# Paired heads in the grouped-query attention, and the squares of the residual norms added on GpSimd ahead of one sum on TensorE

## What is computed

```python
def rmsnorm(x, g):
    y = x * lax.rsqrt(jnp.mean(x * x, axis=-1, keepdims=True) + 1e-6)
    return y * g
...
# 16 query heads, 4 key and value heads, head dimension 64
sc = jnp.einsum('bgrqd,bgkd->bgrqk', qblk, k) * scale
p = jax.nn.softmax(sc, axis=-1)
o = jnp.einsum('bgrqk,bgkd->bgrqd', p, v)
...
x = x + o_all_heads @ w_o
```

## Time and profile before

| | |
|---|---|
| median of 3 runs | 1263.02 us (1260.88 to 1265.97) |
| the profiled execution | 1267.91 us, span 1266.1 us |
| mean granted TensorE clock | 0.963 of 2.4 GHz |
| TensorE matmuls | 1173.1 us busy, 93% of the span, 8610 records |
| VectorE / ScalarE / GpSimd | 764.2 us (60%) / 620.1 us (49%) / 141.3 us (11%) |
| the chain that ended last | TensorE 76%, GpSimd 11%, VectorE 6%, ScalarE 4% |

### The profile page before, as it was taken

How to read it: one execution, slowest core, us unless ns; L and a number is a source line. 1 busy time by engine, 2 the same in 40 slices (tenths; PEclk the granted TensorE clock), 3 DMA queues, 4 the chain that set the end, 5 groups by cost and what they waited for, 6 DMA issues and landing times.

```text
span 1266.1 us, 22011 instructions
## 1 busy us (share of the span) xinstructions
PE 1173.1 (93%) x8610; PEld 1084.8 (86%) x8610; DVE 764.2 (60%) x1164; ACT 620.1 (49%) x1101; POOL 141.3 (11%) x236
## 2 busy tenths in 40 slices
PE   4987879899999999989988899999989999999997
PEld 4876758798999999989955699999978569999997
DVE  3699883355456666546455466656656546656653
ACT  5543325455455545554454355545554455554553
POOL 1399992000000000000000000000000000000000
PEclk8988879899999999999998899999999799999999
DMA  7424112244266665536430066656776104566550
GB/s 244 137 97 150 50 34 81 86 134 133 77 195 171 199 198 171 182 103 183 127 92 1 19 182 177 184 170 168 197 149 143 42 1 135 166 199 193 172 165 33
DMA packets 218142, 169.05 MB, mean 134 GB/s; under 512 B 20787, under 2 KB 208098, under 8 KB 217954
## 3 DMA queue, kind: packets, MB, share of 16 engines
q1 hardware_dynamic: 216962, 164.44, 44.5%
q0 software_dynamic: 496, 2.43, 0.5%
q10 hardware_dynamic: 624, 1.35, 0.4%
HBM read 167.15 MB, written 1.05 MB: 133 GB/s over the span
## 4 chain that ended last, share of the span: by engine, by line
PE 76%; POOL 11%; DVE 6%; ACT 4%; issue 2%; SPq 1%; DMA 1%; DVEq 0%; ACTq 0%; POOLq 0%
PE bank L1847 20%; PE bank L1849 20%; PE bank L1848 20%; PE bank L1913 11%; POOL arena L698 4%; POOL arena L737 2%; DVE wlo L1272 2%; POOL arena L738 1%; ACT whi L766 1%; PE bank L2198 1%; DVE arena L1265 1%; PE bank L1907 1%; PE bank L1909 1%; PE bank L1908 1%; POOL arena L719 1%
## 5 line engine op out<-in xcount | busy, mean ns | idle before, releaser
L1847 PE MATMUL bank<-mem_hi,whi 128*128 128x256 f32 x1408 | 407.4, 289 | 6.5 <-DVE mem_lo L1565 4.9
L1848 PE MATMUL bank<-mem_lo,whi 128*128 128x256 f32 x1408 | 400.4, 284 | 0.0
L1849 PE MATMUL bank<-mem_hi,wlo 128*128 128x256 f32 x1408 | 400.3, 284 | 0.0
L1847 PEld LDWEIGHTS bank<-mem_hi,whi 128*128 128x128 f32 x1408 | 272.2, 193 | 9.2 <-issue 8.5
L1847 PE MATMUL bank<-act_hi,whi 128*128 128x256 f32 (+1 forms) x920 | 267.0, 290 | 12.7 <-DVE act_lo L1291 4.7
L1848 PEld LDWEIGHTS bank<-mem_lo,whi 128*128 128x128 f32 x1408 | 272.0, 193 | 1.9 <-issue 1.4
L1849 PEld LDWEIGHTS bank<-mem_hi,wlo 128*128 128x128 f32 x1408 | 272.0, 193 | 0.0
L1848 PE MATMUL bank<-act_lo,whi 128*128 128x256 f32 (+1 forms) x920 | 261.6, 284 | 0.0
L1849 PE MATMUL bank<-act_hi,wlo 128*128 128x256 f32 (+1 forms) x920 | 261.5, 284 | 0.0
L1272 DVE TENSOR_TENSOR wlo<-raw,whi 128x1024 fp32r<-128x1024 f32 (+3 forms) x137 | 159.0, 1205 | 109.2 <-ACT whi L766 107.7
L1640 DVE TENSOR_TENSOR wlo<-raw,whi 128x1024 fp32r<-128x1024 f32 x177 | 208.9, 1221 | 3.8
(11 more groups left out here) (196 smaller groups left out, 1154.6 us busy)
## 6 DMA issues: line engine op xcount, KB each, us to landing
raw<-in_ffn_w_in_dram SPq DMA_DIRECT2D x132, 512.0 KB, 5.2
raw<-in_ffn_w_out_dram SPq DMA_DIRECT2D x33, 1024.0 KB, 5.0
raw<-in_w_in_ab_dram SPq DMA_DIRECT2D x11, 1024.0 KB, 5.4
raw<-in_w_in_dram SPq DMA_DIRECT2D x9, 1024.0 KB, 7.2
raw<-in_xa_wk_dram SPq DMA_DIRECT2D x4, 1024.0 KB, 5.7
raw<-in_xa_wv_dram SPq DMA_DIRECT2D x4, 1024.0 KB, 5.1
raw<-in_w_out_dram SPq DMA_DIRECT2D x4, 1024.0 KB, 5.0
raw<-in_xa_wq_dram SPq DMA_DIRECT2D x4, 1024.0 KB, 5.0
```

The costliest lines, as they stand in the source:

```text
L1847: pe.matmul(dst, w[0], a[0], start=start, stop=False, **kw)
L1848: pe.matmul(dst, w[0], a[1], start=False, stop=False, **kw)
L1849: return pe.matmul(dst, w[1], a[0], start=False, stop=stop, **kw)
```

## The change

There are two parts, made together.

**Norms 2 to 7.** ScalarE writes the squares of each pair of tiles into the two hf buffers in place of sq. GpSimd adds the four squared pairs into x_sum (three 128x512 additions) and then the halves of x_sum (one 128x256 addition), and TensorE sums that over the partitions by a single 128x256 matmul (`norm_sum`), in place of the eight. It stands behind the second cross-attention query tile (norm 2), behind the fourth k-step of the second half of the first hidden tile (norms 3, 5, 7), right behind the four abreast latent tiles (norm 4), and behind the first query tile (norm 6). GpSimd's load of the late constants stands behind its work for norm 3. In the tails of feed-forwards 0 and 1, VectorE issues x_low of a tile right behind the next tile's addition, not in pairs one pair later.

**Attention.** `attend_pairs` takes the 16 heads as 8 pairs. The score matmuls of the two halves alternate into two of four banks, the value matmuls alternate into the two halves of one bank (6 or 7), the transposes use banks 4 and 5. VectorE scales both heads by one reciprocal and one 1024-wide multiplication. There are four sets of probabilities in an area of their own. Scores of a pair wait for the exponentials of the pair two before it, from the third pair on. `keep_clock` is still issued ahead of the first transposes.

The diff, cut to its core (indentation reduced):

```diff
 grot = room(2, T)
+gprobs = room(4, TT, T, at=0)
+gprobsT = room(4, TT, T)
...
 x_rms_col = sb("x_rms_col", [P, 2, 2])
+x_sum = sb("x_sum", [P, 512])
...
 def score_bank(a):
-    return bank[(a + 2) % 3 if a < 12 else a % 3]
+    return bank[(a + 2) % 3 if a < 12 else a % 4]
...
             step(ins_)
-    pool.wait_ge(s_res, 2 * KC)
+    def add_squares(n):
+        at_ = 4 * (n - 2)
+        half = (x_sum[:, 0:T], x_sum[:, T:2 * T])
+        pool.wait_ge(s_xsq, at_ + 2)
+        if n > 2:
+            pool.wait_ge(s_xss, n - 2)
+        pool.tensor_tensor(x_sum[:], hf[:, 0, :], hf[:, 1, :], ALU.add).then_inc(s_acc, 1)
+        for j in range(2):
+            pool.wait_ge(s_xsq, at_ + 3 + j)
+            pool.wait_ge(s_acc, at_ + 1 + j)
+            pool.tensor_tensor(x_sum[:], x_sum[:], hf[:, j, :], ALU.add).then_inc(s_acc, 1)
+        pool.wait_ge(s_acc, at_ + 3)
+        pool.tensor_tensor(half[0], half[0], half[1], ALU.add).then_inc(s_acc, 1)
+    add_squares(2)
+    add_squares(3)
     pool.dma_start(late, consts[:, early_consts:]).then_inc(s_late, 16)
+    for n in range(4, 8):
+        add_squares(n)
...
         k, ss = stat_no["norm", n], bank[4][:, 0:T]
-        act.wait_ge(s_ss, SQ["norm", n] + 4)
+        act.wait_ge(s_xss, n - 1)
...
            .then_inc(s_hhi, 1)
+    def x_squares(n, j):
+        src = xT[:, 2 * j:2 * j + 2, :].rearrange("p c t -> p (c t)")
+        if n == 8:
+            squares(("norm", n), j, src, 512)
+        else:
+            if j >= 2:
+                act.wait_ge(s_acc, 4 * (n - 2) + j - 1)
+            elif n > 2:
+                act.wait_ge(s_acc, 4 * (n - 3) + 2 + j)
+            act.activation(hf[:, j % 2, :], src, ACT.Square).then_inc(s_xsq, 1)
             if m % 2:
-                squares(("norm", n), m // 2, xT[:, m - 1:m + 1, :].rearrange("p c t -> p (c t)"), 512)
+                x_squares(n, m // 2)
...
         evacuate("gv", i, gv[:, i, :], scale=x_rms_col[:, i, 0:1])
-    attend(12, 16, probs, probsT, GQA_UNITS)
+    def attend_pairs(first, pairs):
+        for i in range(pairs + 3):
+            for half in range(2):
+                a = first + 2 * i + half
+                if i < pairs:
+                    act.wait_ge(s_max, a + 1)
+                    if i >= 2:
+                        act.wait_ge(s_pt, a - 3)
+                    for t in range(TT):
+                        e = act.activation(gprobs[:, a % 4, t, :], score_bank(a)[:, t * T:t * T + T], ACT.Exp,
+                                           bias=nmax[:, a, t:t + 1], accum_out=rsum[:, a, t:t + 1])
+                    e.then_inc(s_exp, 1)
+            for half in range(2):
+                a = first + 2 * (i - 2) + half
+                if 2 <= i < pairs + 2:
+                    act.wait_ge(s_pt, a + 1)
+                    if i >= 4:
+                        act.wait_ge(s_o, a - 3)
+                    act.activation(gprobsT[:, a % 4, :, :],
+                                   bank[4 + a % 2][:].rearrange("p (m t) -> p m t", m=TT), ACT.Copy)\
+                       .then_inc(s_pte, 1)
+            if i >= 3:
+                c = i - 3
+                act.wait_ge(s_o, first + 2 * c + 2)
+                act.activation(act_hi[:, c, :], bank[6 + c % 2][:, 0:T], ACT.Copy).then_inc(s_ohi, 1)
+    attend_pairs(12, 8)
...
                .then_inc(s_res, 1)
-            if n < 8 and m % 2 and m > 1:
-                x_low(n, m - 3)
-                x_low(n, m - 2)
+            if n < 8 and m:
+                x_low(n, m - 1)
         if n < 8:
-            x_low(n, KC - 2)
...
     g_rotate(4)
-    attend(12, 16, probs, GQA_UNITS)
+    def attend_pairs(first, pairs):
+        for i in range(pairs + 4):
+            if i < pairs:
+                for a in range(first + 2 * i, first + 2 * i + 2):
+                    dve.wait_ge(s_score, a + 1)
+                    dve.tensor_reduce(nmax[:, a, :], score_bank(a)[:].rearrange("p (l m) -> p l m", l=TT), AX.X,
+                                      ALU.max, negate=True).then_inc(s_max, 1)
+            if 1 <= i <= pairs:
+                a = first + 2 * i - 2
+                dve.wait_ge(s_exp, a + 2)
+                step(dve.reciprocal(rsum[:, a:a + 2, :], rsum[:, a:a + 2, :]))
+                pr = gprobs[:, a % 4:a % 4 + 2, :, :].rearrange("p h l m -> p (h l) m")
+                r = rsum[:, a:a + 2, :].rearrange("p h l -> p (h l)")
+                mul(pr, pr, r.unsqueeze(2).to_broadcast([P, 2 * TT, T])).then_inc(s_p, 2)
+            if i >= 4:
+                c = i - 4
+                dve.wait_ge(s_ohi, OHI[8 + c])
+                dve.tensor_tensor(act_lo[:, c, :], bank[6 + c % 2][:, 0:T], act_hi[:, c, :].bitcast(F32),
+                                  ALU.subtract).then_inc(s_olo, 1)
+    attend_pairs(12, 8)
...
                     last.then_inc(tile_done, 1)
-            if k >= 3 and k % 2:
-                norm_sums(n, k // 2 - 1)
-        norm_sums(n, 3)
...
                     number == 0, number == 3)
+    def norm_sum(n):
+        pe.wait_ge(s_acc, 4 * (n - 2) + 4)
+        pe.wait_ge(s_rms, 2 * stat_no["norm", n] - 1)
+        plain(bank[4][:, 0:T], ones[:], x_sum[:, 0:T]).then_inc(s_xss, 1)
...
                         last.then_inc(tile_done, 1)
-                    if part and m in (4, 5, 7):
-                        norm_sums(2, {4: 0, 5: 1, 7: 2}[m])
             project(name, m, (name, m // 2), P * (m % 2))
-            if m >= 3 and m % 2:
-                norm_sums(n, m // 2 - 1)
...
             project("xq", 2 * h + k, ("wq", h), P * k, XN, x_first=2 if h == k == 0 else None)
-            if h == k == 0:
-                norm_sums(2, 3)
+            if h == 0 and k == 1:
+                norm_sum(2)
...
                                  (mem_hi[:, k, :], mem_lo[:, k, :]), k == 0, k == KC - 1)
-                if first and j == g == 0:
-                    norm_sums(n, 3)
+                    if first and j == 0 and g == 1 and k == 3:
+                        norm_sum(n)
...
     project_abreast(4, [("lat", i, ("ab", "lat", i // 2), P * (i % 2)) for i in range(4)])
+    norm_sum(4)
...
             if k == 0:
+                if i == 0:
+                    norm_sum(6)
...
     g_swapped(4)
-    def gqa_heads(i):
-        return i // 2, i % 2
-    def gqa_scores(i, b):
-        if i == 0:
+    def gqa_scores(tile, b):
+        if tile == 0:
             evac_wait(pe, "gv", 1)
-        tile, half = gqa_heads(i)
         pe.wait_ge(s_rd, 5 + G_ORDER.index(tile // 2) + 1)
-        r = slice(64 * half, 64 * half + 64)
         for l in range(TT):
-            last = plain(b[:, l * T:l * T + T], gqn[r, tile // 2, tile % 2, l * P:l * P + P],
-                         gqn[r, 4, tile // 4, :])
-        return last
-    def gqa_values(i, b, pT):
-        tile, half = gqa_heads(i)
-        kv = 2 * (tile // 4) + half
+            for half in range(2):
+                r = slice(64 * half, 64 * half + 64)
+                last = plain(b[half][:, l * T:l * T + T], gqn[r, tile // 2, tile % 2, l * P:l * P + P],
+                             gqn[r, 4, tile // 4, :])
+                if l == TT - 1:
+                    last.then_inc(s_score, 1)
+    def gqa_values(tile, b, pT):
         for m in range(TT):
-            last = plain(b[64 * half:64 * half + 64, 0:T], gv[:, m, 64 * kv:64 * kv + 64], pT[:, m, :],
-                         m == 0, m == 1)
-        return last
-    attend(12, 16, gqa_scores, gqa_values, probs, probsT, lambda i: (8 + i // 2, i % 2 == 0),
-           fill=SOFTMAX_FILL)
+            for half in range(2):
+                kv = 2 * (tile // 4) + half
+                last = plain(b[64 * half:64 * half + 64, 0:T], gv[:, m, 64 * kv:64 * kv + 64], pT[half][:, m, :],
+                             m == 0, m == 1)
+                if m == TT - 1:
+                    last.then_inc(s_o, 1)
+    def attend_pairs(first, pairs):
+        for i in range(pairs + 3):
+            if i < pairs:
+                a = first + 2 * i
+                if i >= 2:
+                    pe.wait_ge(s_exp, a - 2)
+                gqa_scores(i, (score_bank(a), score_bank(a + 1)))
+            if 2 <= i < pairs + 2:
+                a = first + 2 * (i - 2)
+                if i == 2:
+                    keep_clock(SOFTMAX_FILL, 6)
+                pe.wait_ge(s_p, a + 2)
+                for half in range(2):
+                    if i >= 3:
+                        pe.wait_ge(s_pte, a + half - 1)
+                    for l in range(TT):
+                        for m in range(TT):
+                            last = pe.transpose(bank[4 + half][:, m * T + l * P:m * T + l * P + P],
+                                                gprobs[:, (a + half) % 4, l, m * P:m * P + P], ident)
+                    last.then_inc(s_pt, 1)
+            if i >= 3:
+                c = i - 3
+                a = first + 2 * c
+                pe.wait_ge(s_pte, a + 2)
+                if c == 1:
+                    pe.wait_ge(s_rd, 10)
+                if c >= 2:
```

(3 more changed lines are left out.)

8 lines of the change are left out of this document (4 added, 4 removed).

## The result

| | before | changed |
|---|---|---|
| median, in the runs taken together | 1264.5 us (1260.9 to 1269.4) | 1245.8 us (1243.3 to 1247.3) |
| profiled execution, its span | 1267.9, 1266.1 | 1245.7, 1243.9 |
| matmul busy | 1173.1 us | 1144.2 us |

The account below looks back on a forecast made before the run. TensorE was taken as the bound. Norms 14.3 us plus attention 13.7 us gave 28.0 us less, from the median of 1263.0 to 1235.0 us; range 1226 to 1250 for 8 in 10, narrower forecast 1229 to 1242.

Parts of the forecast that it names:

- The term 3.04: Each residual norm: eight matmuls become one, taking 3.04 us off TensorE.
- or 351.8 with contention: Norms 3 and 7: GpSimd's adds end at 351.3, or 351.8 with contention; 2.9 us gained at each.
- GpSimd has ended. 3.0 us gained: Norm 2: GpSimd is done before the sum, issued after two query tiles; 3.0 us gained.
- 0.3 us of waiting for the last mem_lo and 0.6 us for GpSimd: Norm 5: these two waits were assumed, leaving 2.1 us gained.
- GpSimd's waits pass 1 us a site: Norms: a sign that would show the forecast wrong; waits under 1 us were expected.
- idles for 1.77: 943.3. Gain 0.: Norm 6: TensorE waits 1.77 us for the key squares behind the moved sum, so nothing is gained.
- fill 5.2: Attention start: the 28 fill records stand on the path and cost 5.2 us, part of it warm.
- 53.5 us for before: Attention: the old code's time from first score to output projection; against 39.8 it gave 13.7 us gained.
- GpSimd locked out by whole weight splits: Rival, norms: whole splits delay GpSimd's last two adds; 14 us back, 1249; chance 7%.
- Clock low through the attention: Rival, attention: the clock stays at 1.2 GHz; 16.7 us of the gain go, 1252; chance 14%.
- Halves that take turns: Rival, attention: alternated halves don't overlap, a pair costs two heads; 1258, or 1279 at low clock; chance 5%.
- No new cost: Rival: no new cost at the attention's start, no wait at norm 6; 17.5 + 18 gives 1227.5; chance 8%.

Follow-up runs that it names:

- experiment 2: The kernel before with the norms' part alone, attention head by head as before: 1251.5 us, ratio 0.9908.
- experiment 6: The changed kernel run again with no edit: 1245.3 us, ratio 0.9854 to the kernel before.
- Experiment 9: The changed kernel with norm 5's weight split behind residual 5 put behind the last residuals: 1242.0 us, ratio 0.9814.
- experiment 1: The kernel before with the paired attention alone, the norms' eight matmuls kept: 1255.6 us, ratio 0.9927.
- experiment 7: The changed kernel with the sum of norm 6 inside the first query tile, behind its fifth k-step: 1240.4 us, ratio 0.9807.
- the second trace: The kernel before, profiled a second time with no edit: 1261.1 us, attention 48.75 us.
- experiment 10: The changed kernel with GpSimd's adds, all but the first, cut to 8 columns in norms 3 to 7: 1247.2 us, ratio 0.9863.
- experiment 4: The changed kernel with its 28 fill records moved ahead of the wait for pair 2's scores: 1242.5 us, ratio 0.9819.
- experiment 5: The changed kernel without the 28 fill records: 1244.0 us, ratio 0.9837.
- combined kernel: The changed kernel with early fill, norm 6's sum inside the first query tile, and norm 5's split behind the last residuals: 1238.7 us, ratio 0.9779.

## Why the prediction was right or wrong

**Norms 2, 3, 4 and 7.** Forecast 12.15 us, 10.5 came. The term 3.04 held: four groups of 0.85 us went, and one matmul of 0.43 came. At 3 and 7 I took 0.76 us for the 256-wide add, "or 351.8 with contention"; it took 1.6 ("the 256 add falls into them" was right, and priced too low), so TensorE waits some 0.3 to 0.4 us. At norm 2 I took "GpSimd has ended. 3.0 us gained", and it had; but 0.6 us came back four tiles later, where the query tile that takes over the bank of tile 0 waits for VectorE's evacuation (L1343). I did not ask what was late next. Norm 4 was right, 3.3.

**Norm 5** was the step that failed among the norms: "0.3 us of waiting for the last mem_lo and 0.6 us for GpSimd". By the spacing of the matmuls' starts in experiments 2 and 6 it was 1.74 us at the sixth k-step and 0.7 more over the next three, and 1.26 at the sum, 3.7 us where 0.9 was forecast. (The brackets in the rows of experiment 2 say 1.57 and 0.99, as a record lasts longer than the 0.12 us to the next start.) The removed matmuls had filled part of the time in which ScalarE and VectorE split weights and made the last residuals; without them the first hidden tile starts (721.19) as VectorE starts a pair of splits (721.33), and residual 6 and mem_lo 5 stand behind that pair. The forecast named the split and gave the wait a size without following the queue up to it. Experiment 9 shows it by moving that one split, which gives 2.2 of the 2.9 us back. By the prediction's own sign, "GpSimd's waits pass 1 us a site", it was wrong at this norm.

**Norm 6.** "idles for 1.77: 943.3. Gain 0." The wait measured 1.83 us. But the stage lost 1.1: I stopped at the first wait. The next one (2.19 in place of 1.42) stands behind ScalarE's chain in the same way, and TensorE had less to do in between, having come to it earlier relative to that chain. A further 1.5 us went in a low-clock stretch behind that idle time, which both traces of the changed kernel have and no trace with the norms of before (both of before, and experiment 1). That the 2.19 us wait causes it was not shown: experiment 7 has the same wait and no such stretch.

**Attention.** Forecast 39.8, measured 38.95 and 39.4. The steps: the wait 985.2 to 990.2, which is 5.0 us, measured 4.92; fill 5.2, measured 4.4 from its start to the transposes; period 3.25, measured 3.29; the halves overlap. What failed is the other side of the subtraction: 53.5 us for before. The 9.9 us at clock 0.50 in the earlier trace rows were one execution's; the second trace and the norms-alone kernel have 48.75. The new code's 38.95 and 39.4 are close to the forecast because the wait, the period and the overlap were right; the fill was 0.8 us shorter than I took it. The gain is 9.5, and attention alone measured 9.2.

**From the profile to the median.** I took the sum off the median (1263.0) though the execution that it was read from was 4.9 us above it, and named this only as an offset. The low clock in the attention costs that execution 4.75 us, about as much as the offset, and I counted it as gain too. (That the two are the same thing wasn't shown: the second execution is 6.8 us shorter, and differs in other stages as well.) It was 22.2 us between the first two profiled executions, 15.4 between the spans of the second trace of before and the first of the changed kernel, which are within 0.1 us of each other up to norm 2, and 18.7 between the medians. The time of 1235.0 missed by 10.8, of which 1.5 is that the median of before is 1264.5 in the later comparison.

**The account:** 8.6 (norms) + 9.5 (attention) = 18.1 of 18.7 us measured. The measured gain itself is known to between 14.9 and 22.6 us, so part of this agreement is luck. Of the missing 9.3: the attention's reference 4.2, norm 5 2.9, norm 6 1.1, norms 2, 3 and 7 1.6, less 0.6 unaccounted. The parts alone gave 9.2 and 11.6, 20.8 in sum (24.1 by the medians), with intervals that hold 18.7.

**The rivals.** GpSimd locked out by whole weight splits (14 us back): no. It gets in between and beside them; the longest wait for it was 1.3 us. The rows of norm 3 say how, with 1.23 us for a split by itself (experiment 10) and 0.76 for the add. The add is issued at 345.66, inside the first split (to 346.66), and ends at 347.25: it waited 0.83 us, less than one split. The second split is issued at 346.58 and takes 1.75, 0.5 longer than alone, as if it began when the add ended. The first had lost 0.24 in the same way to the end of the 512-wide add. The Trainium skill (SBUF — State Buffer, section "SBUF: two separate sides") says that such operations exclude each other for a whole instruction; these rows agree with it to within 0.2 us, and what failed is the rival's step from there to a wait behind both splits. Clock low through the attention: no, it was at 1.00 from 991.35 on. Halves that take turns: no. No new cost: no, the fill and the waits were there. Experiments 4 and 5 show the fill's 4.4 us to be the largest cost that could be avoided, for which I had no proposal. None of the four rivals is what happened; the range held because it was wide enough for them, not because it foresaw the two misses.

## What to carry to other kernels

When work is taken out of the busiest engine, ask at each place what the other engines did meanwhile, and read the next two waits behind the new place from their queues, by name; at norm 5 one weight split ahead of the last residuals cost 2.2 of the 2.9 us by which 2.1 of gain became 0.8 of loss. Filler that is to keep the clock up belongs ahead of the wait that makes the engine idle: behind it, it was on the path here, for 4.4 us. Before a profiled stretch at low clock goes into a difference, look at a second execution, above all where the profile stands above its median: part of what it shows may be the execution's and not the code's.

## What the runs showed of the hardware

**The place of low-clock stretches changes between executions of the same code,** and the time far ahead of the change moves too. The first matmul of `project_tokens` on mem_hi stood at 189.81 us in the second execution of the changed kernel:

```profile
189.81 0.36 PE L1983 MATMUL bank<-whi,mem_hi 128*128 128x256 f32 x1
```

and at 199.60 in the combined kernel, which has the same code up to there:

```profile
199.60 0.36 PE L1985 MATMUL bank<-whi,mem_hi 128*128 128x256 f32 x1
```

In the second trace of before and the first of the changed kernel it stood at 195.10. So single runs are no measure of a 5 us change here. Why one execution falls into one pattern was not found.

**A GpSimd add and VectorE's two-input operations hold each other up.** A 128x256 add took 1.6 us beside a pair of splits, 1.2 beside one split of 640 columns (norm 4 of the changed kernel) and 0.76 in the earlier trace rows; the 128x512 adds, which run mostly beside ScalarE's part of the split, took 1.28 to 1.42. The pair of splits took 3.15 us with the adds beside it and 2.36 without. It shows most on a short operation: at norm 2 of the changed kernel a mem_lo, 0.48 us elsewhere, was issued 0.21 us after a 512-wide add and took 1.36.

```profile
268.90 1.36 DVE L1625 SCALAR_TENSOR_TENSOR mem_lo<-xT,col,mem_hi 128x256 fp32r<-128x256 f32 x1
...
268.69 1.30 POOL L759 TENSOR_TENSOR x_sum<-x_sum,hf 128x512 f32<-128x512 f32 x1 [4.75 <-ACT hf L1057]
```

**After 4.9 us without a matmul TensorE ran at 1.2 GHz, and the clock came back without filler:** in experiment 5 work went on at 980.89, and the eight transposes at 986.68 ran at full speed again, with nothing but scores and transposes between.
